# One more group of modulation columns computed in the recurrence's preparation, one fewer in the first routing stage; the preparation's constants requested by ScalarE

## What is computed

```python
cond_lat = jax.nn.silu(c)
cond_ctx = jax.nn.silu(c_ctx)[None, :]
for layer in range(DEPTH):
    mods_l = jnp.split((cond_lat @ mod_w[layer] + mod_b[layer])[:, None, :], 6, axis=-1)
    mods_c = jnp.split((cond_ctx @ mod_w[layer] + mod_b[layer])[:, None, :], 6, axis=-1)
    hl = modulate(rms_norm(x), mods_l[0], mods_l[1])
```

## Time and profile before

| What | us |
|---|---|
| median of three executions | 4473.89 |
| the profiled execution's own time | 4474.47 |
| its span, first to last instruction | 4472.7 |
| second preparation stage: first instruction of it to first of the next | 766.63 to 848.91 |
| first routing stage: first instruction of it to first of the next | 1839.82 to 1911.84 |

### The profile page before, as it was taken

One profiled execution on the slowest core, in us unless ns is written; L12 is line 12 of the kernel. 1 busy time (PEld: TensorE's weight loads), 2 busy tenths in 40 slices (PEclk: granted clock), 3 DMA queues, 4 the chain that ended last, 5 costly groups with the idle time before them and its releaser, 6 DMA issues. The chain is left out here.

```text
span 4472.7 us, 88140 instructions
## 1 busy us (share of the span) xinstructions
PE 3745.6 (84%) x34494; PEld 2428.8 (54%) x34495; DVE 1867.3 (42%) x4520; ACT 1373.7 (31%) x3101; POOL 576.5 (13%) x898
## 2 busy tenths in 40 slices
PE   3998996698988959679999926998999795999992
PEld 1886553488888837423333305896666582333331
DVE  3322554677777656400000045424777653000004
ACT  2211564366666322011111102113666520111111
POOL 0000000034444323000000020100000010000001
PEclk6999998799999979689999967999999896999996
DMA  6221002422222244489997883214000234899984
GB/s 247 71 86 73 10 10 79 151 60 79 68 78 73 58 133 156 166 350 364 389 375 311 323 312 108 86 65 156 10 11 10 89 123 181 340 360 400 412 355 178
DMA packets 250474, 772.07 MB, mean 173 GB/s; under 512 B 76624, under 2 KB 164688, under 8 KB 219056
## 3 DMA queue, kind: packets, MB, share of 16 engines
q1 hardware_dynamic: 200624, 646.00, 38.6%
q10 hardware_dynamic: 36144, 72.89, 4.3%
q0 software_dynamic: 13392, 48.76, 2.8%
HBM read 642.16 MB, written 117.54 MB: 170 GB/s over the span
## 5 line engine op out<-in xcount | busy, mean ns | idle before, releaser
L3372 PE MATMUL ex_bY<-ex_w,ex_aT 128*64 x880 | 390.8, 597 | 51.0 <-DVE ex_aT L3437 46.2
L3372 PE MATMUL ex_bG<-ex_w,ex_xT 128*64 x880 | 392.3, 599 | 17.3 <-DMA ex_w<-in_moe_w_gate 17.3
L3372 PE MATMUL ex_bU<-ex_w,ex_xT 128*64 x880 | 390.5, 597 | 7.6 <-DMA ex_w<-in_moe_w_up 7.6
L3373 PE MATMUL ex_bG<-ex_w,ex_xT 128*64 128x512 f32 x880 | 392.3, 599 | 0.0
L3373 PE MATMUL ex_bY<-ex_w,ex_aT 128*64 128x512 f32 x880 | 391.1, 597 | 0.0
L3373 PE MATMUL ex_bU<-ex_w,ex_xT 128*64 128x512 f32 x880 | 390.5, 597 | 0.0
L3435 DVE TENSOR_TENSOR ex_a<-ex_sg,ex_bU 128x512 f32<-128x512 f32 x55 | 37.9, 689 | 771.8 <-PE ex_bU L3373 771.8
L3372 PEld LDWEIGHTS ex_bY<-ex_w,ex_aT 128*64 128x64 f32 x880 | 116.4, 137 | 278.5 <-issue 278.5
L3372 PEld LDWEIGHTS ex_bG<-ex_w,ex_xT 128*64 128x64 f32 x880 | 121.6, 139 | 268.4 <-issue 268.4
L3372 PEld LDWEIGHTS ex_bU<-ex_w,ex_xT 128*64 128x64 f32 x880 | 121.2, 138 | 258.0 <-issue 258.0
L1037 DVE TENSOR_SCALAR_CACHE_REDUCE ad_p<-ad_S 128x512 f32<-128x512 f32 (+1 forms) x384 | 215.6, 600 | 100.0 <-PE ad_S L947 100.0
(11 more groups left out here) (493 smaller groups left out, 8596.4 us busy)
## 6 DMA issues: line engine op xcount, KB each, us to landing
ex_w<-in_moe_w_gate SPq DMA_DIRECT2D x65, 2048.0 KB, 11.7
ex_w<-in_moe_w_up SPq DMA_DIRECT2D x65, 2048.0 KB, 14.8
ex_w<-in_moe_w_down SPq DMA_DIRECT2D x65, 2048.0 KB
yb_dram<-ex_y ACTq DMA_DIRECT2D x55, 512.0 KB, 10.2
rm_mw<-in_mod_w SPq DMA_DIRECT2D x16, 1024.0 KB, 8.1
rt_mw<-in_mod_w SPq DMA_DIRECT2D x16, 1024.0 KB, 8.2
kb_dram<-rs_pout SPq DMA_DIRECT2D x60, 256.0 KB, 2.7
rs_KB<-kb_dram SPq DMA_DIRECT2D x120, 128.0 KB, 2.7
```

The lines of the kernel that those rows point to most:

```text
L3372: nc.tensor.matmul(bank[0:BR, :], stationary[:, k, 0:BR], w[:, ds(slot + (offset + k * n), 512)], start=k == 0, stop=k == total - 1)
L3373: m = nc.tensor.matmul(bank[BR:P, :], stationary[:, k, BR:P], w[:, offset + k * n:offset + k * n + 512], start=k == 0, stop=k == total - 1)
```

## The change

Group (1, 1) moves from the routing stage to the preparation, whose ring grows to five slices. In the shared stage five slices and twelve bias transfers are requested instead of four and eight. In the second stage SyncE requests slices 5 and 6 directly after the inputs, ahead of the 14 small transfers, and all later slices directly after those; `load_constants` now stands at the head of ScalarE's stream. TensorE does products 3 and 4, the transposes, product 5, the norm and gate matmuls, products 6 to 17, `srk`, and then products 18 to 23. VectorE does the third `add` behind `const.columns`. The routing stage keeps one group: eight slices, four bias transfers, one `add` and four stores.

```diff
-FIRST_GROUPS, NORM_GROUPS, PREP_GROUPS, ROUTE_GROUPS = [(0, 0)], [(0, 1)], [(0, 2), (1, 0)], [(1, 1), (1, 2)]
-PREP_EARLY = 3
+FIRST_GROUPS, NORM_GROUPS, PREP_GROUPS, ROUTE_GROUPS = [(0, 0)], [(0, 1)], [(0, 2), (1, 0), (1, 1)], [(1, 2)]
+PREP_RING, PREP_EARLY = 5, 3
...
-    def __init__(self, nc, s, d, groups, banks):
+    def __init__(self, nc, s, d, groups, banks, ring=MRING):
+        self.ring = ring
...
-        if n >= MRING:
-            sp.wait_ge(self.used, n - MRING + 1)
+        if n >= self.ring:
+            sp.wait_ge(self.used, n - self.ring + 1)
...
-                for n in range(MRING):
+                for n in range(PREP_RING):
                     mods.load(sp, n)
                 mods.load_bias(sp)
...
                     load_padded(sp, x[:, i, :], projT[A_COLS + c0:A_COLS + c0 + P, :], x_in)
+                for n in range(PREP_RING, PREP_RING + 2):
+                    mods.load(sp, n)
...
                 sp.dma_start(ind[:, :], d["headcols"]).then_inc(c_in, 16)
-                for n in range(MRING, MRING + 2):
-                    mods.load(sp, n)
-                const.load_constants(sp)
-                for n in range(MRING + 2, mods.n):
+                for n in range(PREP_RING + 2, mods.n):
                     mods.load(sp, n)
...
-                for n in range(PREP_EARLY, MRING + 1):
+                for n in range(PREP_EARLY, PREP_RING):
                     mods.product(pe, sil, n)
...
-                mods.product(pe, sil, MRING + 1)
+                mods.product(pe, sil, PREP_RING)
...
-                for n in range(MRING + 2, mods.n):
+                for n in range(PREP_RING + 1, mods.n - 6):
                     mods.product(pe, sil, n)
                 dv.wait(pe, "rk")
...
                 pp.did("srk", mm)
+                for n in range(mods.n - 6, mods.n):
+                    mods.product(pe, sil, n)
 
             @block.scalar
             def _(act):
+                const.load_constants(act)
                 for b in range(3):
                     pp.wait(act, f"vt{b}")
...
-                for g in range(len(PREP_GROUPS)):
+                for g in range(len(PREP_GROUPS) - 1):
                     mods.add(dve, g)
...
                 const.columns(dve)
+                mods.add(dve, len(PREP_GROUPS) - 1)
...
-        mods = None if sil is None else Mods(nc, s, d, ROUTE_GROUPS, [s.ps("macc0"), s.ps("macc1")])
+        mods = None if sil is None else Mods(nc, s, d, ROUTE_GROUPS, [s.ps("macc0")])
...
-                    mods = Mods(nc, s, d, PREP_GROUPS, bank[6:8])
+                    mods = Mods(nc, s, d, PREP_GROUPS, [bank[6], bank[7], bank[3]], ring=PREP_RING)
```

More of the change, by code:

```diff
@@ L83 @@
 MRING = 4
-FIRST_GROUPS, NORM_GROUPS, PREP_GROUPS, ROUTE_GROUPS = [(0, 0)], [(0, 1)], [(0, 2), (1, 0)], [(1, 1), (1, 2)]
-PREP_EARLY = 3
+FIRST_GROUPS, NORM_GROUPS, PREP_GROUPS, ROUTE_GROUPS = [(0, 0)], [(0, 1)], [(0, 2), (1, 0), (1, 1)], [(1, 2)]
+PREP_RING, PREP_EARLY = 5, 3
 class Mods:
-    def __init__(self, nc, s, d, groups, banks):
+    def __init__(self, nc, s, d, groups, banks, ring=MRING):
+        self.ring = ring
         self.nc, self.d, self.groups, self.banks = nc, d, groups, banks
         self.n = KT * len(groups)
-        self.w = s.sb("mw", [P, MRING, MG])
+        self.w = s.sb("mw", [P, self.ring, MG])
         self.bias = self.rows = s.sb("mbias", [P, len(groups), 512])
-        self.w_in = [s.sem(f"mw_in{u}") for u in range(MRING)]
+        self.w_in = [s.sem(f"mw_in{u}") for u in range(self.ring)]
         self.cleared, self.bias_in, self.used, self.added, self.out = (s.sem(n) for n in ("mcleared", "mbias_in", "mused", "madded", "mout"))
@@ L109, in load @@
     def load(self, sp, n):
-        if n >= MRING:
-            sp.wait_ge(self.used, n - MRING + 1)
+        if n >= self.ring:
+            sp.wait_ge(self.used, n - self.ring + 1)
         l, c = self.groups[n // KT]
         src = self.d["mod_w"][l].rearrange("(p k) n -> p k n", k=KT)
-        sp.dma_start(self.w[:, n % MRING, :], src[:, n % KT, c * MG:(c + 1) * MG]).then_inc(self.w_in[n % MRING], 16)
+        sp.dma_start(self.w[:, n % self.ring, :], src[:, n % KT, c * MG:(c + 1) * MG]).then_inc(self.w_in[n % self.ring], 16)
     def product(self, pe, sil, n):
-        pe.wait_ge(self.w_in[n % MRING], 16 * (n // MRING + 1))
+        pe.wait_ge(self.w_in[n % self.ring], 16 * (n // self.ring + 1))
         k = n % KT
         for v in range(4):
-            x = self.nc.tensor.matmul(self.banks[n // KT][32 * v:32 * v + 32, :], sil[:, k, :], self.w[:, n % MRING, v * 512:(v + 1) * 512], start=k == 0, stop=k == KT - 1)
+            x = self.nc.tensor.matmul(self.banks[n // KT][32 * v:32 * v + 32, :], sil[:, k, :], self.w[:, n % self.ring, v * 512:(v + 1) * 512], start=k == 0, stop=k == KT - 1)
         x.then_inc(self.used, 1)
```

## The result

The changed kernel has a median of 4489.18 us over eight executions (4484.45 to 4496.11), the kernel before 4475.30 over eight beside them. The ratio is 1.0032 with a 95% interval of 1.0022 to 1.0042: slower by 13.9 us. That lies in the stated range, but outside the most likely case: the forecast was +5.6 us, no change that shows, and the measured change is clear of 0.2%.

The account below looks back on a forecast made before the run. TensorE is busy for 84% of the span, but each changed stage ends with its last stream: modulation work in routing, one chain in the preparation. +18.0 - 12.4 = +5.6 us gave 4480.1 us (4479.5 against the median), range 4467 to 4492.

Parts of the forecast that it names:

- the most likely case: Whole kernel: preparation 18.0 us longer, routing stage 12.4 shorter, sum +5.6 us, no change that shows; chance 0.57.
- the pace of the burst: Preparation: ScalarE's 52 requests for constants at SyncE's 0.50 us each, so ScalarE is free at 797.0, 8.7 us late.
- The bound of 1.15 us: Preparation: upper end for one constants request on ScalarE; the 52 would then take 60 us.
- the forecast's own range: Whole kernel: 4472 to 4486 us, from the bounds of clock, landing and pace (0.43 to 0.56 us per request).
- Rival 1: Preparation: SyncE and ScalarE hold each other's requests up, ScalarE free 12 us later, at 809; 4491.5 us; chance 0.20.
- ScalarE held: Preparation: ScalarE does nothing else while requesting constants, so its copies of the transposes come 8.7 us late.
- TensorE's clock: Preparation: after some 10 us without work TensorE runs the norm matmuls at a lower clock, 2.1 us longer (0 to 2.4).
- The wait of 4.48 us gone: Preparation: VectorE's idle time at the first `add`, for products 14 and 15, vanishes; `ksum` is 6.3 us later than before.
- the gate matmuls without effect: Preparation: the twelve may be slower, but VectorE meets their results only after its long reciprocal; nothing put on it.
- The tail behind `srk`: Preparation's end: six products left, slice 23 landing 6.0 us after its request; next stage at 866.9, bounds -1.5 and +5.
- The routing stage: With one group its last work is the sum right behind the routing chain: 12.4 us shorter, bounds 11.2 and 12.4.
- so the 1.2 us come through: Routing stage: four bias requests fewer ahead of the slices bring products and the rank matmuls behind them 1.2 us sooner.

Follow-up runs that it names:

- e9_products_between_gates: Changed kernel with constants spread over SyncE's spare time, products 6 to 9 between gate matmuls, no product behind `srk`: 0.9984 against the kernel before, 4464.51 us.

## Why the prediction was right and where it was off

**The failed term is the pace of the burst.** "I take SyncE's 0.50, as these are the same transfers": it was 0.68 us per request, 9.4 us more in all. The text gave the exchange rate (5.2 us per 0.1 us) and the point from which the sum is slower by over 0.2%, 0.56 us, so the outcome follows from the sum once this term is put right: 5.6 + 9.4 = 15.0, against 15.6 in the two stages (the tail 0.9 shorter, the routing stage's gain 1.5 smaller) and 13.9 between the medians. The bound of 1.15 us held, but the forecast's own range stopped at 0.56. Its listed bounds also add up to 4483.9 at the upper end and not to 4486; 4489.18 lies above either. What I missed is in the change itself: on SyncE the constants stood behind two slices, and most of them went out with next to nothing moving; in the new order ScalarE asks for them while slices 5 to 10 are on their way. Busy time and clock by stretch, columns as in the earlier trace rows, the last the GB/s moved, for SyncE's burst before in two parts and for ScalarE's in the changed kernel:

```profile
781.36:788.00 6.64, 2.75 (x12) 1.09 (x13) 6.43 (x9) 0.00 (x0) 0.00 (x0) 0.50 0.98 355
788.00:807.32 19.32, 14.65 (x46) 6.07 (x44) 15.78 (x8) 14.84 (x22) 0.00 (x0) 0.98 0.27 27
```

```profile
770.10:805.45 35.35, 3.70 (x18) 2.19 (x18) 12.81 (x16) 0.00 (x0) 0.00 (x0) 0.59 0.95 246
```

**Rival 1 has nearly the right size for the wrong reason.** It put the burst's end 12 us late by mutual hold-up of the issuers; it was 9.4 late. The stated range reaches to 4492 for this rival's sake alone, so that the time lies in it is in part luck. The run without slices in flight leaves at most 1.2 us for the hold-up, and requests are held where only one engine asks. The rule of the Trainium skill behind it (Perfetto Trace Analysis, section "DMA Instruction — HWDGE (DVE, Sync)": one descriptor block, locked for one sequencer at a time) may hold, but two issuers in turn are not what sets the time here. The other one (DMA: Bandwidth & Descriptors, section "Issuing engines are not separate DMA queues": all issuers' transfers run on the same 16 engines and interleave) is what the trace agrees with: 5.9 us to landing with slices under way, 2.1 without. Its remark that the time on the sequencer is usually small beside the transfer holds for one request of 0.45 us with 2.1 to landing; 52 in a row held ScalarE for 35.4 us.

**ScalarE held:** right. Its copies follow the last request at once, and with the constants back on SyncE the chain is 20.6 us earlier in the stage.

**TensorE's clock:** right. The norms took 4.64 us after 14.2 us without a matmul, 2.2 more, for 2.1 forecast; the granted clock in them was 0.50, the 1.2 GHz level. With the constants back on SyncE they follow product 5 without a pause (789.14) and took 2.42 again, at 1.00.

**The wait of 4.48 us gone, the gate matmuls without effect:** right, in every run with a late chain.

**The tail behind `srk`:** 12.4 us for 13.3 forecast. The last slice was asked for at 863.94 and its product started at 869.10, 5.2 us for the 6.0 assumed. Without four of its products it is 7.8.

**The routing stage:** -10.9 for -12.4. The step that failed is "so the 1.2 us come through". The first slice was there 1.2 us sooner, the second and third took 3.06 and 3.09 us instead of 2.41 and 2.49, and the fourth product stood where it had stood. The other runs with four bias requests show the same (fourth product at 17.44 to 17.72). Why is open; no run tried it. Of the other 0.3 us most lies ahead of the sum: it stands 57.31 us into the stage instead of 57.05.

## What to carry to other kernels

Requests moved to a compute engine are work at the head of its stream, and their price is not what the old issuer paid: it grows when large transfers are under way at that moment, on SyncE as on ScalarE. Before such a move, look whether the old issuer has time to spare further down (here SyncE had 40 us with one request in them, from 786.0 until product 6, started at 824.89, had made room in the ring at 826.0). Work that is moved out of one stage should be placed in the next so that its transfers' requests don't wait for the stage's last result: six products behind the last matmul cost about what the stage that they left had gained.

## What was not expected of the hardware

- The same small request takes 0.45 us or up to 4.24 on ScalarE. The long ones come in the stretches in which slices are moving, and SyncE's requests are held in them too when it is the only one that asks (2.09 and 1.53 us at 787.43 and 789.56 with spread constants). Beside ScalarE's burst SyncE's own small requests also rose, to 1.84 and 2.13 us at 777.72 and 779.60. What the request waits for (room in a queue, or something else) no run shows.
- Slices with four small transfers behind each came at 3.3 us per MiB, those behind the last small one at 2.5 (`e9_products_between_gates`).
- GpSimd asks for these transfers at 0.58 us each, hardly slower than SyncE's 0.50. The small transfers that the transposes wait for then land 26.9 us into the stage (793.95), against 24.6 in the changed kernel (790.25).
